# Wide and narrow products of one chunk in turns: the order of a four-step block of matmuls

## The chip, the cores and the metric

The kernel runs on one core of a Trainium2 chip. The metric is the device time of one launch in microseconds (us), the median of several runs. The profile is of one execution of the same program; its own time is given beside its span.

## The reference

Two transformer-like blocks are applied to 256 tokens of width 2048, in float32. The part that matters here is that nearly all of the work is products of a weight matrix with the activations:

```
# first block                              # second block
proj = h @ w_in            (2048 -> 3072)  proj = h @ w_in_2           (2048 -> 11264)
y = concat(y_lru, y_pool) @ w_out          merged = sig_r * (o_ret @ w_ret_up) + sig_m * (o_moba @ w_moba_up)
x = x + gt1 * y                            x = x + merged @ w_out_2
f = (silu(h @ w_ffn_gate)                  f = gated, convolved (h @ w_ffn_up_2)
     * (h @ w_ffn_up)) @ w_ffn_down             @ w_ffn_down_2
x = x + gt2 * f                            x = x + f ; final norm
```

Between them lie norms, a modulation from a vector c (`c_act @ w_ada`), a short convolution, a gated recurrence, a pooling mixer, and in the second block retention and block attention over the same 256 tokens. The feed-forward width is 5632.

## The kernel before

Activations are feature-major: a tile such as `h_s` is 128 partitions x 16 blocks x 2 halves x 256 tokens. The two halves are the high part of a number in the fp32r format (half 0) and the rest of it (half 1). Weights are treated the same way: each weight is split into a high and a low part, and a product of a weight with an activation is taken as high x high, high x low and low x high.

**Slabs and chunks.** A weight matrix is worked on in slabs of 256 output columns. A slab is two blocks of 128 columns (`b` = 0, 1), and its contraction is cut into four chunks of `kt` blocks of 128 (`kt` is 4, and 3 in the last group of the feed-forward down-projection). SP's queue loads the chunk into `raw`. ACT writes its high part into the tile `split` (`convert`, L902), DVE subtracts and writes the low part (L1241) and counts up `lo_ready`. `split` is a ring of four slots; ACT waits for `chunk_used`, which the last product of a chunk counts up, before it writes over a slot.

**Products.** `multiply` does one chunk. The accumulator is `ps[:, s, b, :]`: slab parity `s` and block `b` select one of four PSUM banks of 512 numbers. For each k and b there are two products. The *wide* one has the high weights as its stationary operand and both halves of the activations as its 512 moving columns; it writes the whole bank. The *narrow* one has the low weights and the high half of the activations, 256 columns, and writes the first half of the same bank. After the slab ACT copies the second half out (L909) and DVE adds it to the first (L1254, L1256). In the slabs of values (`tok`, L560 and L567) weights and activations change places.

Before, a step of k is: wide of block 0, wide of block 1, narrow of block 0, narrow of block 1:

```
for b in range(2):
    pe.matmul(ps[:, s, b, :], ...512 columns..., start=start, stop=False)
for b in range(2):
    mm = pe.matmul(ps[:, s, b, 0:T], ...256 columns..., start=False, stop=stop)
```

**Who calls it.** `half_slab` (first projection, two chunks at a time), `slab` (nearly everything), the merge loop of the second block (moving operands `o_r` and `o_m`), and `first_pair`, the first two slabs of the first feed-forward part: there PE waits before each k for `h_ready`, since the activations are normalized block by block on DVE and ACT (L1370, L1375) while the products already run. All others wait ahead of a chunk. The last slab before each of two norms is done by `closing` (L648 to L650) instead, which has three narrow products for each k and b, all to one bank: in chunks 0 to 2 b changes after every three, in the last chunk all of block 0 come first. `closing` is not touched. Between chunks `ride_along` puts in products of the modulation (L591, L599, L611).

Of the kernel before, what the change touches and what calls it, by code (L numbers as in the profile page):

```python
# [29 lines left out]
P = 128  # L30
T = 256
D = 2048
DB = D // P
SLAB = 256
# [105 lines left out]
def build(nc, dram, out):  # L140
# [3 lines left out]
    def at(name, shape, offset, dt=F32):  # L144
        return nc.alloc_sbuf_tensor_at(name, shape, dt, offset=offset)

    top = 16512
    def place(size):
        nonlocal top
        where, top = top, top + size  # L150
        return where

    raw = at("raw", [P, RAW, KT, SLAB], place(RAW * KT * SLAB * 4))
    split = at("split", [P, RING, KT, 2, SLAB], place(RING * KT * 2 * SLAB * 4), F32R)
# [91 lines left out]
    ps = ctx.enter_context(nc.psum_tensor("ps", [P, 2, 2, 512], F32))  # L246
# [289 lines left out]
    def _(pe):  # L536
        def slab(S, s, acts, kt=KT, guard=None, tok=False, rides=False, after=None):

            if not (isinstance(S, int) and S < 2):
                pe.wait_ge(evacuated, evac_count_of(S) - 1)  # L540
            for c in range(CHUNKS):
                if guard is not None:
                    guard(c)
                multiply(CHUNKS * S + c, c, s, acts, c * kt, kt, c == 0, c == CHUNKS - 1, tok)
                if rides:
                    ride_along(CHUNKS * S + c)
                if after is not None:
                    after(c)

        def multiply(G, slot, s, acts, k0, kt, first, last, tok=False, ready=None):  # L550


            pe.wait_ge(lo_ready, G + 1)
            for k in range(kt):
                if ready is not None:
                    pe.wait_ge(h_ready, ready + k + 1)
                start, stop = first and k == 0, last and k == kt - 1
                for b in range(2):
                    if tok:
                        pe.matmul(ps[:, s, b, :], acts[:, k0 + k, 0, b * P:(b + 1) * P],  # L560
                                  split[:, slot, k, :, :].rearrange("p h n -> p (h n)"), start=start, stop=False)
                    else:
                        pe.matmul(ps[:, s, b, :], split[:, slot, k, 0, b * P:(b + 1) * P],  # L563
                                  acts[:, k0 + k, :, :].rearrange("p h t -> p (h t)"), start=start, stop=False)
                for b in range(2):
                    if tok:
                        mm = pe.matmul(ps[:, s, b, 0:SLAB], acts[:, k0 + k, 1, b * P:(b + 1) * P],  # L567
                                       split[:, slot, k, 0, :], start=False, stop=stop)
                    else:
                        mm = pe.matmul(ps[:, s, b, 0:T], split[:, slot, k, 1, b * P:(b + 1) * P],  # L570
                                       acts[:, k0 + k, 0, :], start=False, stop=stop)
            mm.then_inc(chunk_used, 1)

        offset = [HALF_SLABS]
# [141 lines left out]
        def half_slab(E, after=None):  # L716

            if E >= 2:
                pe.wait_ge(evacuated, E - 1)
            for c in range(2):  # L720
                k0 = KT * (2 * (E // HALF_SLABS) + c)
                if E % HALF_SLABS == 0:
                    pe.wait_ge(h_ready, k0 + KT)
                multiply(2 * E + c, (2 * E + c) % RING, E % 2, h_s, k0, KT, c == 0, c == 1)
                ride_along(2 * E + c)
# [24 lines left out]
        def first_pair(gu):  # L750

            for i in range(2 * CHUNKS):
                G, s, c = CHUNKS * gu + i, i % 2, i // 2
                if c == 0:
                    pe.wait_ge(evacuated, evac_count_of(gu + s) - 1)
                multiply(G, G % RING, s, h_s, c * KT, KT, c == 0, c == CHUNKS - 1,
                         ready=DB + c * KT if s == 0 else None)
# [93 lines left out]
        for q in range(IN2_SLABS):  # L851
# [4 lines left out]
            if q == 2:  # L856
# [3 lines left out]
                for b in range(2):  # L860
                    mm = pe.matmul(pm[3][:, b:b + 1], rstd_h[:, b * P:(b + 1) * P], ident[:, 0:1], start=True, stop=True)
# [1155 lines left out]
```

## Time and profile before

| | |
|---|---|
| median of 3 runs | 2596.44 us (2596.14 to 2596.61) |
| the profiled execution | 2596.39 us |
| its span | 2594.3 us |
| PE busy | 2527.9 us, 97% |
| weight loads (PEld) | 2147.6 us, 83% |
| DVE, ACT busy | 1781.3 us (69%), 1179.6 us (45%) |
| DMA | mean 214 GB/s |

PE is TensorE's matmul row and PEld its weight-load row; every matmul has a weight load of its own. Starts of matmuls are recorded, their ends are modelled, so the time from one start to the next tells how fast they go, and durations don't. Rows of several instructions give the start of the first.

### The profile page before, as it was taken

The page shows a single profiled execution, that of the slowest core. Times are in us where ns is not written, and L with a number is a line of the kernel's source. Part 1 is how long each engine was busy: PE and PEld are TensorE (multiplying, and loading weights), DVE is VectorE, ACT ScalarE, POOL GpSimd, SP SyncE. Part 2 cuts the span into 40 slices and gives each one's busy share as a digit, 9 for nine tenths or more (in the row PEclk, how much of TensorE's full clock was granted, in tenths as well). Part 3 has the DMA queues.
Part 4 walks back from the last instruction along what each step waited for, and adds up shares of the span by engine and source line. Part 5 has one row for each costly group of instructions (what it writes and reads, how often), then busy time and mean ns, then how long its engine had stood idle before and what let it go on. Part 6 is the DMA issues. An engine that isn't in the chain of part 4 may idle for free.

```text
span 2594.3 us, 39845 instructions
## 1 busy us (share of the span) xinstructions
PE 2527.9 (97%) x14556; PEld 2147.6 (83%) x14556; DVE 1781.3 (69%) x2300; ACT 1179.6 (45%) x1439; POOL 17.5 (1%) x52
## 2 busy tenths in 40 slices
PE   4999999999999999999999999999999999999998
PEld 0666788888888888888888888888888888888887
DVE  2568698955555555688686665576788668876886
ACT  1345345444444444564454554445544444444444
POOL 1000000000000000000000000000000000000000
PEclk8999999999999999999999999999999999999999
DMA  9978987955555555566555455556555655555554
GB/s 372 402 273 325 381 336 261 355 179 190 191 186 187 191 188 186 165 194 201 188 172 172 163 176 188 188 184 195 177 181 184 204 185 192 186 189 181 190 167 125
DMA packets 156809, 554.48 MB, mean 214 GB/s; under 512 B 16400, under 2 KB 20496, under 8 KB 156704
## 3 DMA queue, kind: packets, MB, share of 16 engines
q1 hardware_dynamic: 155376, 549.85, 61.8%
q0 software_dynamic: 1328, 3.21, 0.4%
q8 instruction: 68, 1.11, 0.2%
q14 instruction: 37, 0.30, 0.0%
HBM read 550.37 MB, written 2.10 MB: 213 GB/s over the span
## 4 chain that ended last, share of the span: by engine, by line
PE 90%; DVE 4%; DMA 3%; ACT 1%; issue 1%; SPq 0%; DVEq 0%; ACTq 0%
PE ps L563 55%; PE ps L570 27%; DMA ride<-in_w_ada 3%; PE ps L560 2%; PE pm L591 2%; DVE split L1241 1%; PE ps L567 1%; ACT split L902 1%; DVE acc_out L1294 0%; PE pm L611 0%; DVE x_t L1397 0%; PE pm L712 0%; DVE val L1254 0%; DVE val L1370 0%; DVE h_s L1596 0%
## 5 line engine op out<-in xcount | busy, mean ns | idle before, releaser
L1241 DVE TENSOR_TENSOR split<-raw,split 128x1024 fp32r<-128x1024 f32 (+1 forms) x864 | 1030.8, 1203 | 686.1 <-ACT split L902 682.6
L902 ACT ACTIVATE split<-raw 128x1024 fp32r<-128x1024 f32 (+1 forms) x864 | 896.1, 1043 | 1138.7 <-PE ps L570 1081.0
L563 PE MATMUL ps<-h_s,split 128*128 128x512 f32 x3880 | 1231.0, 399 | 14.3 <-DVE split L1241 6.4
L570 PEld LDWEIGHTS ps<-h_s,split 128*128 128x128 f32 x3880 | 731.1, 188 | 173.0
L570 PE MATMUL ps<-h_s,split 128*128 128x256 f32 x3880 | 764.6, 278 | 0.0
L563 PE MATMUL ps<-mid_s,split 128*128 128x512 f32 x2336 | 737.3, 397 | 0.5 <-DVE split L1241 0.4
L563 PEld LDWEIGHTS ps<-h_s,split 128*128 128x128 f32 x3880 | 594.5, 189 | 43.0 <-issue 35.7
L570 PEld LDWEIGHTS ps<-mid_s,split 128*128 128x128 f32 x2336 | 440.2, 188 | 104.2
L570 PE MATMUL ps<-mid_s,split 128*128 128x256 f32 x2336 | 460.0, 278 | 0.0
L563 PEld LDWEIGHTS ps<-mid_s,split 128*128 128x128 f32 x2336 | 356.7, 189 | 7.4 <-issue 5.2
L909 ACT ACTIVATE low<-ps 128x512 f32<-128x512 f32 x230 | 133.2, 579 | 0.0
L591 PE MATMUL pm<-ride,c_act 128*1 128x512 f32 x512 | 75.9, 667 | 36.1 <-DMA ride<-in_w_ada 36.1
L1254 DVE TENSOR_TENSOR val<-ps,low 128x512 f32<-128x512 f32 x126 | 86.1, 683 | 1.2 <-ACT low L909 1.1
L1682 DVE SCALAR_TENSOR_TENSOR conv_o<-up_pad,par,conv_o 128x256 f32<-128x256 f32 x176 | 77.5, 482 | 11.4 <-DVE conv_o L1680 5.6
L560 PE MATMUL ps<-split,h_s 128*128 128x512 f32 x256 | 80.9, 397 | 0.0
L1256 DVE TENSOR_TENSOR low<-ps,low 128x512 f32<-128x512 f32 x88 | 60.2, 684 | 0.2
L591 PEld LDWEIGHTS pm<-ride,c_act 128*1 128x1 f32 x512 | 6.8, 81 | 62.6 <-DMA ride<-in_w_ada 37.4
L567 PEld LDWEIGHTS ps<-split,h_s 128*128 128x128 f32 x256 | 48.1, 188 | 11.4
L567 PE MATMUL ps<-split,h_s 128*128 128x256 f32 x256 | 50.3, 278 | 0.0
L1100 ACT ACTIVATE conv_o<-conv_o 128x512 f32<-128x512 f32 x22 | 13.9, 634 | 65.4 <-DVE conv_o L1682 65.4
L563 PE MATMUL ps<-o_m,split 128*128 128x512 f32 x128 | 40.3, 396 | 0.0
L563 PE MATMUL ps<-o_r,split 128*128 128x512 f32 x128 | 40.2, 395 | 0.0
(267 smaller groups left out, 1196.3 us busy)
## 6 DMA issues: line engine op xcount, KB each, us to landing
raw<-in_w_in SPq DMA_DIRECT2D x224, 512.0 KB, 3.5
ride<-in_w_ada SPq DMA_DIRECT2D x64, 1024.0 KB, 8.3
raw<-in_w_ffn_down SPq DMA_DIRECT2D x128, 512.0 KB, 4.2
raw<-in_w_ffn_gate SPq DMA_DIRECT2D x88, 512.0 KB, 4.2
raw<-in_w_ffn_up SPq DMA_DIRECT2D x88, 512.0 KB, 4.2
raw<-in_w_ffn_a SPq DMA_DIRECT2D x88, 512.0 KB, 3.7
raw<-in_w_ffn_b SPq DMA_DIRECT2D x88, 512.0 KB, 4.4
raw<-in_w_out SPq DMA_DIRECT2D x64, 512.0 KB, 5.4
```

The costliest lines, as they stand in the source:

```text
L560: pe.matmul(ps[:, s, b, :], acts[:, k0 + k, 0, b * P:(b + 1) * P], split[:, slot, k, :, :].rearrange("p h n -> p (h n)"), start=start, sto ...
L563: pe.matmul(ps[:, s, b, :], split[:, slot, k, 0, b * P:(b + 1) * P], acts[:, k0 + k, :, :].rearrange("p h t -> p (h t)"), start=start, sto ...
L567: mm = pe.matmul(ps[:, s, b, 0:SLAB], acts[:, k0 + k, 1, b * P:(b + 1) * P], split[:, slot, k, 0, :], start=False, stop=stop)
L570: mm = pe.matmul(ps[:, s, b, 0:T], split[:, slot, k, 1, b * P:(b + 1) * P], acts[:, k0 + k, 0, :], start=False, stop=stop)
L591: mm = pe.matmul(pm[2 + n % 2][g:g + 1, :], c_act[:, k:k + 1], src[:, e, 512 * h:512 * h + 512], start=(i == 0), stop=(i == PIECES - 1))
L902: act.activation(split[:, c, 0:kt, 0, :], raw[:, CHUNKS * s + c, 0:kt, :], ACT.Copy).then_inc(hi_ready, 1)
L909: act.activation(low[:, s, :, :], ps[:, s, :, T:2 * T], ACT.Copy).then_inc(low_copied, 1)
L1100: act.activation(conv_o[:, 0, :, :], conv_o[:, 0, :, :], ACT.Silu).then_inc(act_done, 1)
L1241: dve.tensor_tensor(split[:, c, 0:kt, 1, :], raw[:, CHUNKS * s + c, 0:kt, :], split[:, c, 0:kt, 0, :].bitcast(F32), ALU.subtract).then_inc ...
L1254: ins = dve.tensor_tensor(dst, ps[:, s, :, 0:T], both, ALU.add)
L1256: own(dve.tensor_tensor(both, ps[:, s, :, 0:T], both, ALU.add))
L1682: ins = dve.scalar_tensor_tensor(out=dst, in0=src, scalar=w, in1=dst, op0=ALU.mult, op1=ALU.add)
```

## The change

In a chunk, the order of the same products. One loop over k takes the wide product of block 0 and the narrow one of block 1; a second loop takes the wide product of block 1 and the narrow one of block 0. The wide product that opens a bank's sum (`start`) must come before any narrow one to that bank, so in the first chunk of a slab the wide one of block 1 for k = 0 is taken ahead of everything, and in the second loop the wide ones of block 1 run one k ahead (`k + 1`), with none beside the last narrow one. `mm.then_inc(chunk_used, 1)` stays on the chunk's last product. The waits for `h_ready` are in the first loop only.

```
+            def wide(b, k):
+                start, stop = first and k == 0, last and b == 1 and k == kt - 1
+                ...
+            def narrow(b, k):
+                stop = last and b == 0 and k == kt - 1
+                ...
             for k in range(kt):
                 if ready is not None:
                     pe.wait_ge(h_ready, ready + k + 1)
-                start, stop = first and k == 0, last and k == kt - 1
-                for b in range(2):
-                    ...wide...  start=start, stop=False
-                for b in range(2):
-                    ...mm = narrow...  start=False, stop=stop
+                if k == 0 and first:
+                    wide(1, 0)
+                wide(0, k)
+                narrow(1, k)
+            for k in range(kt):
+                if not first:
+                    wide(1, k)
+                elif k + 1 < kt:
+                    wide(1, k + 1)
+                mm = narrow(0, k)
             mm.then_inc(chunk_used, 1)
```

With W for wide, N for narrow and the block behind it, four k of a later chunk go from `W0 W1 N0 N1` four times to `W0 N1` four times and then `W1 N0` four times; a slab's first chunk becomes `W1 W0 N1 W0 N1 W0 N1 W0 N1 W1 N0 W1 N0 W1 N0 N0`.

## Rows read from the trace of the kernel before

**Rows 1.** The page: busy times, the chain that ended last, the converts of DVE

```profile
PE 2527.9 (97%) x14556; PEld 2147.6 (83%) x14556; DVE 1781.3 (69%) x2300; ACT 1179.6 (45%) x1439; POOL 17.5 (1%) x52
...
PE 90%; DVE 4%; DMA 3%; ACT 1%; issue 1%; SPq 0%; DVEq 0%; ACTq 0%
PE ps L563 55%; PE ps L570 27%; DMA ride<-in_w_ada 3%; PE ps L560 2%; PE pm L591 2%; DVE split L1241 1%; PE ps L567 1%; ACT split L902 1%; DVE acc_out L1294 0%; PE pm L611 0%; DVE x_t L1397 0%; PE pm L712 0%; DVE val L1254 0%; DVE val L1370
...
L1241 DVE TENSOR_TENSOR split<-raw,split 128x1024 fp32r<-128x1024 f32 (+1 forms) x864 | 1030.8, 1203 | 686.1 <-ACT split L902 682.6
```

**Rows 2.** Waits of PE: total us, times, longest us

```profile
PE pm L591 <- DMA ride<-in_w_ada: 36.1, 18, 19.5
PE ps L563 <- DVE split L1241: 6.8, 3, 6.1
...
PE ps L563 <- DVE h_s L1375: 2.5, 1, 2.5
```

**Rows 3.** Stretches: busy us of each engine (instructions), granted clock, DMA share, GB/s

```profile
600.00:1000.00 400.00, 400.00 (x2299) 349.02 (x2299) 228.51 (x240) 175.40 (x191) 0.00 (x0) 1.00 0.57 189
...
396.00:399.00 3.00, 3.00 (x10) 2.52 (x11) 3.00 (x9) 2.03 (x4) 0.00 (x0) 0.50 0.37 143
```

**Rows 4.** Groups of PE by line and form: count, busy us, mean ns, idle before

```profile
L563 PE MATMUL ps<-h_s,split 128*128 128x512 f32 x3880 | 1231.0, 399 | 14.3 <-DVE split L1241 6.4 <-issue 3.1 <-DVE h_s L1375 2.5
L570 PE MATMUL ps<-h_s,split 128*128 128x256 f32 x3880 | 764.6, 278 | 0.0
L563 PE MATMUL ps<-mid_s,split 128*128 128x512 f32 x2336 | 737.3, 397 | 0.5 <-DVE split L1241 0.4
...
L560 PE MATMUL ps<-split,h_s 128*128 128x512 f32 x256 | 80.9, 397 | 0.0
...
L563 PE MATMUL ps<-o_m,split 128*128 128x512 f32 x128 | 40.3, 396 | 0.0
L563 PE MATMUL ps<-o_r,split 128*128 128x512 f32 x128 | 40.2, 395 | 0.0
```

**Rows 5.** PE in order of time, steady stretch: start us, us, what

```profile
1600.14 0.63 PE L563 MATMUL ps<-h_s,split 128*128 128x512 f32 x2
1600.61 0.39 PE L570 MATMUL ps<-h_s,split 128*128 128x256 f32 x2
1600.84 0.63 PE L563 MATMUL ps<-h_s,split 128*128 128x512 f32 x2
...
1611.29 0.63 PE L563 MATMUL ps<-h_s,split 128*128 128x512 f32 x2
```

**Rows 6.** PE in order of time at the lower clock

```profile
397.23 1.05 PE L563 MATMUL ps<-h_s,split 128*128 128x512 f32 x2
398.09 0.63 PE L570 MATMUL ps<-h_s,split 128*128 128x256 f32 x2
398.51 1.05 PE L563 MATMUL ps<-h_s,split 128*128 128x512 f32 x2
```

**Rows 7.** Single products and weight loads of one step, in order of time

```profile
1499.65 0.40 PE L563 MATMUL ps<-h_s,split 128*128 128x512 f32 x1
...
1499.88 0.19 PEld L570 LDWEIGHTS ps<-h_s,split 128*128 128x128 f32 x1
...
1499.88 0.40 PE L563 MATMUL ps<-h_s,split 128*128 128x512 f32 x1
1500.12 0.28 PE L570 MATMUL ps<-h_s,split 128*128 128x256 f32 x1
1500.12 0.19 PEld L570 LDWEIGHTS ps<-h_s,split 128*128 128x128 f32 x1
...
1500.23 0.19 PEld L563 LDWEIGHTS ps<-h_s,split 128*128 128x128 f32 x1
...
1500.35 0.62 PE L563 MATMUL ps<-h_s,split 128*128 128x512 f32 x2
```

**Rows 8.** The closing slab of the end: first and last products of 72

```profile
2572.77 0.28 PE L648 MATMUL ps<-h_s,split 128*128 128x256 f32 x1
2572.89 0.28 PE L649 MATMUL ps<-h_s,split 128*128 128x256 f32 x1
...
2581.28 0.28 PE L650 MATMUL ps<-h_s,split 128*128 128x256 f32 x1
```

**Rows 9.** The merge loop, steps that read o_m: first and eighth

```profile
1667.72 0.63 PE L563 MATMUL ps<-o_m,split 128*128 128x512 f32 x2
...
1672.66 0.63 PE L563 MATMUL ps<-o_m,split 128*128 128x512 f32 x2
```

**Rows 10.** DVE in order of time while first_pair begins

```profile
395.18 0.48 DVE L1375 SCALAR_TENSOR_TENSOR h_s<-val,mod,h_s 128x256 fp32r<-128x256 f32 x1 [0.18 <-ACT h_s L967]
...
395.98 0.48 DVE L1375 SCALAR_TENSOR_TENSOR h_s<-val,mod,h_s 128x256 fp32r<-128x256 f32 x1
...
396.76 0.48 DVE L1375 SCALAR_TENSOR_TENSOR h_s<-val,mod,h_s 128x256 fp32r<-128x256 f32 x1
...
397.55 0.48 DVE L1375 SCALAR_TENSOR_TENSOR h_s<-val,mod,h_s 128x256 fp32r<-128x256 f32 x1
```

More of the change, by code:

```diff
@@ L553, in multiply @@
             pe.wait_ge(lo_ready, G + 1)
+            def wide(b, k):
+                start, stop = first and k == 0, last and b == 1 and k == kt - 1
+                if tok:
+                    return pe.matmul(ps[:, s, b, :], acts[:, k0 + k, 0, b * P:(b + 1) * P],
+                                     split[:, slot, k, :, :].rearrange("p h n -> p (h n)"), start=start, stop=stop)
+                return pe.matmul(ps[:, s, b, :], split[:, slot, k, 0, b * P:(b + 1) * P],
+                                 acts[:, k0 + k, :, :].rearrange("p h t -> p (h t)"), start=start, stop=stop)
+            def narrow(b, k):
+                stop = last and b == 0 and k == kt - 1
+                if tok:
+                    return pe.matmul(ps[:, s, b, 0:SLAB], acts[:, k0 + k, 1, b * P:(b + 1) * P],
+                                     split[:, slot, k, 0, :], start=False, stop=stop)
+                return pe.matmul(ps[:, s, b, 0:T], split[:, slot, k, 1, b * P:(b + 1) * P],
+                                 acts[:, k0 + k, 0, :], start=False, stop=stop)
             for k in range(kt):
@@ L556, in multiply @@
                     pe.wait_ge(h_ready, ready + k + 1)
-                start, stop = first and k == 0, last and k == kt - 1
-                for b in range(2):
[L559 to L564, printed above, removed]
-                for b in range(2):
[L566 to L571, printed above, removed]
+                if k == 0 and first:
[8 more added lines that the diff above has]
+                mm = narrow(0, k)
             mm.then_inc(chunk_used, 1)
```

## The prediction

> **What bounds the kernel now.** I read the page first. TensorE is busy for 97% of the span and makes 90% of the chain that ended last, and nearly all of that chain is the lines of `multiply`: L563 and L570, and L560 and L567 for the token-major slabs [rows 1]. The waits of PE come next. The longest total is 36.1 us on the DMA of the early modulation weights; waits for a split chunk come to 6.8 us, and for a normalized block to 2.5 us [rows 2]. None is inside the long stretch: between 600 and 1000 us PE is busy for all 400 us at granted clock 1.00 [rows 3]. So the time is set by how fast TensorE takes one product after another, and I look at the starts of products, because their ends are modelled.
>
> The change acts on wide products (512 columns) and narrow ones (256). The grouped lines give 3880 + 2336 + 128 + 128 + 256 = 6728 wide ones and as many narrow ones [rows 4], so there are 3364 steps of k with two wide and two narrow products each. In the steady stretch a pair of wide ones starts at 1600.14, its pair of narrow ones at 1600.61, and the pair of wide ones 16 steps on at 1611.29: 11.15 / 16 = 0.697 us a step, 0.47 of it for the wide pair and 0.23 for the narrow pair [rows 5]. 3364 x 0.697 = 2345 us of the 2594.3 us span lies in such steps. The smallest change that a measurement can tell from none, 0.2% or 5.2 us, is 5.2 / 3364 = 1.5 ns a step. The question is whether the order moves a step of 697 ns by 1.5 ns.
>
> **What a step is made of.** At the start of the first feed-forward part the granted clock is 0.50 [rows 3], the 1.2 GHz level, and there the step takes 398.51 - 397.23 = 1.28 us [rows 6]. At the 2.4 GHz level half of that, 640 ns, would be its pure column work; it takes 697. So 57 ns a step are not column work, 14 for each product. Where in the order do they sit? Two views help. The single starts show a weight load with each product, and each load starts when the product before it starts (loads at 1499.88, 1500.12 and 1500.23, in each case at the start of a product) [rows 7]: one load ahead, never two. The other view is the closing slab, which is narrow products only: 71 intervals from 2572.77 to 2581.28 make 8.51 / 71 = 0.120 us each [rows 8], which is 107 of column work (a sixth of 640 ns: 256 of 1536 columns) and 13 more. That row also holds the bank question: there three products in a row write one bank, and in the last chunk twelve do, at the same 0.12 us. Four products at 13 ns make 53 of the 57. About 4 ns a step (between 3 and 5 by the rounding of these rows) are peculiar to the mixed step, and these can hang on order.
>
> **The change, part by part.**
> *Instructions.* The same 16 products of a chunk of four k, with the same operands, starts and stops and the same single signal at the end: 14556 matmuls before and after. Nothing is removed or added. 0 us.
>
> *Banks.* The title says that neighbours shall write different banks. They do already: before, the order is bank 0, 1, 0, 1 in every step and across steps. After, they alternate inside each of the two loops, but the narrow one of block 1 that ends the first loop is followed in a later chunk by a wide one of block 1, and the chunk ends on block 0 where the next chunk of the slab begins; in a slab's first chunk the last two narrow ones both write block 0. So same-bank neighbours rise from none to two or so a chunk. By the closing slab such a neighbour costs nothing [rows 8]. I take 0 us; as a bound, even 4 ns on each of 2 x 856 neighbours would be 6.8 us (864 converted chunks [rows 1], less the eight of the two closing slabs, which don't use `multiply`).
>
> *Loads.* Before, the loads under a step's four products are those of a wide, narrow, narrow and wide one; all are 128x128. After, each wide product covers the load of a narrow one and each narrow one that of a wide one. Both orders have two loads a step under wide products (0.235 us each) and two under narrow ones (0.115). With one load ahead [rows 7] and all loads alike, the sum is the same. 0 us.
>
> A rule bears on this: the Trainium skill, "TensorE: Matmul & The Clock Gate", section "Back-to-back issue gap", gives a warm isolated product its columns over 2.4 GHz and about 2.5 ns, whatever stands beside it. An estimate from that page is 650 ns for a step in either order; the trace disagrees with the size (697) and says nothing against the independence of order. By the page the sum is again 0 us.
>
> *Width changes.* Before, a step has two changes of width (wide to narrow, narrow to wide) and after it four. The trace of before holds all four kinds of neighbours. Starts are 0.23 after a wide one that follows narrow, 0.24 after the wide one ahead of narrow, 0.11 to 0.12 after a narrow one [rows 7]; the kind of neighbour moves an interval by no more than the 10 ns that a row can show. So it isn't excluded that the 4 ns peculiar to the mixed step belong to one kind. If they belong to the wide products as such, 0. If to the two width changes, they double: +4 x 3364 = +13.5 us. If to a wide one behind a wide one, or to a narrow one behind a narrow one in the mixed step, they go: -13.5 us. I take the first, because each product's load and columns are what they were, and the rows show the wide interval as 0.23 to 0.24 in both surroundings.
>
> *Addresses.* One row shows that a step can depend on what else it reads: with o_m as the moving operand, seven steps take 1672.66 - 1667.72 = 4.94, or 706 ns each [rows 9], 9 more than with h_s. The new order pairs other loads with other moving operands, so up to 9 x 3364 = 30 us bounds this from above. The two tiles h_s and mid_s, with which nearly all steps run, show no such thing in either pair of a step, so I take 0.
>
> *Blocks that arrive one by one.* Only `first_pair` waits inside a chunk. After, the second half of a chunk runs behind the last wait. There DVE finishes a block every 0.79 us (395.18, 395.98, 396.76, 397.55) [rows 10], and the clock is at 1.2 GHz. After, the first loop takes 1.07 us for k = 0 (two wide ones at a third of 1.28, 0.427, and a narrow one at a sixth, 0.213) and 0.64 for each further one: it would want k = 1 to 3 at 396.9, 397.5 and 398.2, and they are there by about 396.5, 397.2 and 398.0 (start plus 0.48). PE doesn't wait. 0 us, at most 0.1. Elsewhere the waits come ahead of the whole chunk. The converts on ACT and DVE wait for a chunk's last product, which stays where it was; so do the copies out of `ps`.
>
> Sum: 2594.3 + 0 of the span, and the profiled execution, 2596.39, stands 2.1 above its span and at the median of the runs, 2596.44. Forecast 2596.5.
>
> **The rivals.**
> *No effect (forecast), 2596.5; own range 2591 to 2602.* For it: same loads, same columns, one load ahead, alternating banks before. This is also the case in which the change doesn't do what it says. Chance 0.52.
>
> *Width changes cost, 2610.* The mixed step's 4 ns sit at the two changes of width and become 8. For it: the interval ahead of the narrow pair is the longest wide one, 0.24 [rows 7]; a queue that has just loaded under a short product may start the long one late. Against it: narrow to wide is no longer than narrow to narrow. It decides from 1.5 ns a step. With the address effect on top it could reach 2626. Chance 0.22.
>
> *Spacing out the narrow ones helps, 2583.* With two narrow products in a row, two loads running lie under short products; in turns, each load under a short product comes after one under a long product, in which the queue can get ahead. For it: loads back to back all the way, as in the closing slab, run at 0.120 an interval where the mixed step's narrow pair has 0.115 each, so a narrow product does go faster after wide ones [rows 5, 8]. A gain of 4 ns a step is 13.5 us. If each narrow interval fell to the shortest shown, 0.11, it would be 2 x 5 x 3364 = 34 us, 2563. Against it: the total of a step need not fall when a start moves. Chance 0.26.
>
> **How the numbers follow.** The three cases are also the three outcomes, since each rival's price is over twice the 0.2%: same 0.52, slower 0.22, faster 0.26. The range takes in both rivals at their 13.5 us with some 2 to 3 us for the rounding of the 4 ns: 2580 to 2613. Outside are the extremes, the address effect and narrow intervals at their floor, about 1 in 10 each.
>
> **What would show it right or wrong.** Right: 16 steps of k in the steady stretch again take 11.15 us, whatever the order inside; wide intervals 0.23 to 0.24, narrow ones 0.115; ACT and DVE wait for PE as before. The slower rival shows as wide intervals of 0.24 throughout or narrow ones of 0.12, with every chunk of four k longer than 2.79 us. The faster one shows as narrow intervals of 0.11 at the same wide ones. If bank neighbours mattered, the interval at a chunk's middle and end would stand out from the rest. The prediction is wrong if the step's 57 ns depend on which product a load lies under, which no row of before can show, since its order is the same everywhere.

## The result and the profile after

The changed kernel takes 2609.33 us (median of 5 runs, 2608.06 to 2611.08), against 2596.44 for the kernel before (5 runs, 2595.33 to 2596.80): a ratio of 1.0047, with a 95% interval of 1.0036 to 1.0058. It is slower by about 13 us. The time lies in the range of the prediction and beside the 2610 us of its slower rival. The case that the prediction held to be the likeliest, no effect, did not come.

The page after, beside [rows 1]:

```profile
span 2607.8 us, 39845 instructions
...
PE 2542.6 (97%) x14556; PEld 2155.6 (83%) x14556; DVE 1781.5 (68%) x2300; ACT 1180.9 (45%) x1439; POOL 17.4 (1%) x52
```

The number of products is the same, and the other engines work as long as before. Only PE has more. Its waits, beside [rows 2], haven't grown:

```profile
PE pm L604 <- DMA ride<-in_w_ada: 34.9, 17, 20.3
PE ps L561 <- DVE split L1254: 6.7, 3, 6.1
...
PE ps L561 <- DVE h_s L1388: 2.5, 1, 2.5
```

So nobody keeps PE waiting longer. The stretches, beside [rows 3], at the same granted clock:

```profile
600.00:1000.00 400.00, 400.00 (x2284) 348.35 (x2283) 227.33 (x241) 173.83 (x188) 0.00 (x0) 1.00 0.57 187
```

PE gets 2284 products done in the 400 us where it did 2299: 0.66% fewer. The loss is in the intervals themselves, and it is not spread evenly. PE in order of time, at the starts of three slabs (the two wide products in a row mark a slab's first chunk):

```profile
743.01 0.63 PE L561 MATMUL ps<-h_s,split 128*128 128x512 f32 x2
...
754.15 0.63 PE L561 MATMUL ps<-h_s,split 128*128 128x512 f32 x2
...
765.45 0.63 PE L561 MATMUL ps<-h_s,split 128*128 128x512 f32 x2
...
967.41 0.63 PE L561 MATMUL ps<-h_s,split 128*128 128x512 f32 x2
```

One slab takes 11.14 us and the next 11.30. Before, 16 steps take 11.15 [rows 5]. The 20 slabs from 743.01 to 967.41 average 11.22. Inside the first of the two, in a later chunk, eight pairs of a wide and a narrow product, that is four steps of k, go by in 2.77 us (746.18 to 748.95). Inside the second they take 2.83 us (759.43 to 762.26):

```profile
746.18 0.39 PE L561 MATMUL ps<-h_s,split 128*128 128x512 f32 x1
...
748.95 0.39 PE L561 MATMUL ps<-h_s,split 128*128 128x512 f32 x1
...
759.43 0.40 PE L561 MATMUL ps<-h_s,split 128*128 128x512 f32 x1
759.68 0.28 PE L569 MATMUL ps<-h_s,split 128*128 128x256 f32 x1
759.80 0.40 PE L561 MATMUL ps<-h_s,split 128*128 128x512 f32 x1
760.03 0.28 PE L569 MATMUL ps<-h_s,split 128*128 128x256 f32 x1
760.14 0.40 PE L561 MATMUL ps<-h_s,split 128*128 128x512 f32 x1
760.38 0.28 PE L569 MATMUL ps<-h_s,split 128*128 128x256 f32 x1
760.50 0.40 PE L561 MATMUL ps<-h_s,split 128*128 128x512 f32 x1
...
762.26 0.40 PE L561 MATMUL ps<-h_s,split 128*128 128x512 f32 x1
```

The same alternation of the same products on the same tiles has two rhythms. In the fast one a step takes 2.77 / 4 = 0.693 us, less than the 0.697 of before. In this chunk of the slow one it takes 0.708. The rows are rounded to 0.01 us, but the trace holds the starts to 1 ns: the slow rhythm goes in a cycle of three pairs, with wide intervals of 241, 235 and 234 ns and narrow ones of 121, 113 and 116; in the fast one wide intervals are 230 to 233 ns and narrow ones 112 to 117. What puts a slab into one or the other is the matter of the experiments.

### The profile page after: what moved, and what is told of

Its sections match the earlier page's. It is cut to its first block, busy times and chain, and to the rows that moved or that the text cites. A ratio compares the mean times of both kernels' runs of the same rounds, so it can differ in the third digit from the quotient of the medians.

```text
span 2607.8 us, 39845 instructions
## 1 busy us (share of the span) xinstructions
PE 2542.6 (97%) x14556; PEld 2155.6 (83%) x14556; DVE 1781.5 (68%) x2300; ACT 1180.9 (45%) x1439; POOL 17.4 (1%) x52
## 4 chain that ended last, share of the span: by engine, by line
PE 92%; DVE 3%; DMA 3%; issue 1%; ACT 1%; SPq 0%; DVEq 0%; ACTq 0%
PE ps L561 55%; PE ps L569 28%; DMA ride<-in_w_ada 3%; PE ps L559 2%; PE pm L604 2%; PE ps L567 1%; DVE acc_out L1307 1%; DVE split L1254 1%; ACT split L915 0%; PE pm L624 0%; PE pm L725 0%; PE pm L612 0%; PE ps L661 0%; DVE val L1267 0%; PE ps L662 0%
## 5 line engine op out<-in xcount | busy, mean ns | idle before, releaser
L561 PE MATMUL ps<-h_s,split 128*128 128x512 f32 x3880 | 1368.9, 400 | 14.2 <-DVE split L1254 6.4
L569 PE MATMUL ps<-h_s,split 128*128 128x256 f32 x3880 | 1067.6, 281 | 0.0
L561 PEld LDWEIGHTS ps<-h_s,split 128*128 128x128 f32 x3880 | 724.7, 189 | 204.9 <-issue 37.5
L561 PE MATMUL ps<-mid_s,split 128*128 128x512 f32 x2336 | 815.9, 397 | 0.3 <-DVE split L1254 0.3
L569 PEld LDWEIGHTS ps<-h_s,split 128*128 128x128 f32 x3880 | 735.7, 190 | 12.0
L569 PE MATMUL ps<-mid_s,split 128*128 128x256 f32 x2336 | 641.8, 280 | 0.0
L561 PEld LDWEIGHTS ps<-mid_s,split 128*128 128x128 f32 x2336 | 433.6, 188 | 105.4 <-issue 6.0
L569 PEld LDWEIGHTS ps<-mid_s,split 128*128 128x128 f32 x2336 | 441.1, 189 | 6.9
L559 PE MATMUL ps<-split,h_s 128*128 128x512 f32 x256 | 89.8, 398 | 0.0
L567 PE MATMUL ps<-split,h_s 128*128 128x256 f32 x256 | 70.3, 280 | 0.0
L559 PEld LDWEIGHTS ps<-split,h_s 128*128 128x128 f32 x256 | 47.6, 188 | 10.7
L567 PEld LDWEIGHTS ps<-split,h_s 128*128 128x128 f32 x256 | 48.3, 189 | 0.7
```

Of the source, the lines that this page charges most:

```text
L559: return pe.matmul(ps[:, s, b, :], acts[:, k0 + k, 0, b * P:(b + 1) * P], split[:, slot, k, :, :].rearrange("p h n -> p (h n)"), start=sta ...
L561: return pe.matmul(ps[:, s, b, :], split[:, slot, k, 0, b * P:(b + 1) * P], acts[:, k0 + k, :, :].rearrange("p h t -> p (h t)"), start=sta ...
L567: return pe.matmul(ps[:, s, b, 0:SLAB], acts[:, k0 + k, 1, b * P:(b + 1) * P], split[:, slot, k, 0, :], start=False, stop=stop)
L569: return pe.matmul(ps[:, s, b, 0:T], split[:, slot, k, 1, b * P:(b + 1) * P], acts[:, k0 + k, 0, :], start=False, stop=stop)
```

## The experiments

In all of them but the last two, `multiply` walks through a list `plan` of (wide or narrow, block, k), with the same calls `wide` and `narrow`, the same `start` on the first product of each bank's sum and the signal on the chunk's last product. Only the list is shown. Each time is the median of 4 to 11 runs (one for `wideonly`), and its ratio is to 17 to 33 runs of the kernel before in the same session; one execution of each was profiled. A step's length is read from starts of products in the steady stretch; its loss is what it has above 693.3 ns, for a reason that `wideonly` gives.

**1. Alternate without a break (pairs).**

```diff
+plan = [(kind, b, k) for k in range(kt) for b in range(2) for kind in "wn"]      # W0 N0 W1 N1
```

> Order in every chunk W0 N0 W1 N1 for each k: wide and narrow alternate without a break, also across first chunks, and each pair writes one bank. After shows two rhythms of the alternating order, some 693.5 and some 707.5 ns per step of k, that change from slab to slab where the first chunk has two wide and two narrow ones in a row. Two-rhythm theory: with no such seam one rhythm stays, so nearly all slabs are fast (about 2596.5 - 3364 x 3.2 ns = 2586 us) or nearly all slow (about 2596.5 + 3364 x 10.8 ns = 2633 us), not half and half. Width-change theory (2 ns for each change of width, four a step): 2610 us, every step about 701 ns. Bank theory (after lost its 13 us at some 2.5 same-bank neighbours a chunk, 6 ns each): two such neighbours a step, 2596.5 + 3364 x 2 x 6 ns = 2637 us.

2607.01 us (2598.26 to 2618.36), ratio 1.0032 (1.0017 to 1.0047). The spread is the finding: 20 us between runs, where before has 5.4 in the same sessions. The profiled execution took 2618.36 us and is slow for the whole stretch from 600 to 1000 us:

```profile
600.00:1000.00 400.00, 400.00 (x2266) 346.83 (x2265) 225.78 (x238) 171.81 (x186) 0.00 (x0) 1.00 0.56 185
```

That is 1.4% fewer products than before, every slab alike: by starts to 1 ns, all 142 whole chunks of four k in this stretch take 705 to 708 ns a step, 706.7 on average. The change from slab to slab is gone with the two wide and two narrow ones in a row. This also answers a rival: the other engines' work differs between the two slabs of a pair (in the changed kernel 8 DVE instructions from 743.0 to 754.1 us, 5 from 754.1 to 765.4), and here both kinds of slab keep one rhythm. One rhythm for a whole run, 2586 or 2633, was expected too, and that didn't come.

**2. The same, banks as in the change (noseam).**

```diff
+k0_ = 1 if first else 0
+plan = [(kind, b, 0) for b in range(2) for kind in "wn"] if first else []
+plan += [p for k in range(k0_, kt) for p in (("w", 0, k), ("n", 1, k))]
+plan += [p for k in range(k0_, kt) for p in (("w", 1, k), ("n", 0, k))]
```

> As the changed kernel, but a slab's first chunk begins W0 N0 W1 N1 for k = 0 and then goes on W0 N1 and W1 N0, so there are never two of one width in a row; same-bank neighbours stay a few a chunk. Two-rhythm theory: no switching from slab to slab; 2586 us if the rhythm that stays is the fast one, 2633 us if the slow one. Width-change theory: 2610 us. Bank theory: 2610 us as well, since the count of same-bank neighbours hardly changes.

2603.44 us (2596.68 to 2616.78), ratio 1.0021 (1.0012 to 1.0031), again with a spread of 20 us. The profiled execution (2616.78 us) shows why. Its stretches:

```profile
600.00:1000.00 400.00, 400.00 (x2267) 346.93 (x2266) 226.00 (x240) 172.70 (x187) 0.00 (x0) 1.00 0.56 185
...
1800.00:2020.00 220.00, 219.59 (x1242) 190.16 (x1242) 173.58 (x241) 105.75 (x126) 0.00 (x0) 1.00 0.55 184
2320.00:2500.00 180.00, 180.00 (x1040) 157.38 (x1039) 126.77 (x167) 78.85 (x86) 0.00 (x0) 1.00 0.57 189
```

and those of before:

```profile
1800.00:2020.00 220.00, 219.51 (x1260) 191.38 (x1259) 178.02 (x251) 105.58 (x124) 0.00 (x0) 1.00 0.55 185
2320.00:2500.00 180.00, 180.00 (x1036) 157.04 (x1035) 130.37 (x176) 78.85 (x86) 0.00 (x0) 1.00 0.55 181
```

The first two stretches are slow from end to end (2267 products for 2299, 1242 for 1260). The last is fast, faster than before (1040 for 1036). So a rhythm holds for hundreds of microseconds and changes at a few places in a run. What changes it there is not known. That the spread of both kernels' runs comes from which rhythm is held for how long fits the profiled executions, which are the slowest of their ten runs; the faster runs have no trace.

**3. Banks alone (samebank).**

```diff
+plan = [p for k in range(kt) for p in (("w", 0, k), ("w", 1, k), ("n", 1, k), ("n", 0, k))]
```

> The order before with its narrow ones exchanged: W0 W1 N1 N0 for each k. Widths in the same order as before, but two same-bank neighbours a step (W1 N1, N0 W0) where before had none. Bank theory: 2637 us, or at least clearly above 2600. Two-rhythm and width-change theory: banks don't matter, 2596.5 us.

2597.48 us (2594.25 to 2599.32), ratio 0.9997 (0.9987 to 1.0006). Two same-bank neighbours in every step cost nothing that these runs or the traces show; the step is 696.7 ns in both. The bank theory falls, and with it the aim that the prediction names for the change ("neighbours shall write different banks"): there was nothing to gain from different banks.

**4. Fewer changes of width (fours).**

```diff
+plan = [(kind, b, k) for j in range(0, kt, 2) for kind in "wn" for k in range(j, min(j + 2, kt)) for b in range(2)]
```

> Two k together: W0 W1 W0 W1 N0 N1 N0 N1, always alternating banks, half as many changes of width as before (one a step). Width-change theory: 2596.5 - 3364 x 2 ns = 2590 us. Bank theory: 2596.5 us. Two-rhythm theory: no forecast of the size; narrow ones in a row drift toward the closing slab's 0.120 us, so up to 3364 x 4 ns = 13 us slower, 2600 to 2610 us.

2608.47 us (2607.49 to 2608.83), ratio 1.0043 (1.0029 to 1.0057). Half the changes of width, and as slow as the change under study. A price for each change of width, whatever stands around it, is out. PE in order of time:

```profile
804.47 1.09 PE L567 MATMUL ps<-h_s,split 128*128 128x512 f32 x4
805.40 0.64 PE L575 MATMUL ps<-h_s,split 128*128 128x256 f32 x4
...
808.68 1.09 PE L567 MATMUL ps<-h_s,split 128*128 128x512 f32 x4
```

Six steps take 4.21 us, 0.702 each, of which four wide ones take 0.93 and four narrow ones 0.48, that is 0.12 apiece as in the closing slab [rows 8].

**5. Wide products by themselves (wideonly).** The narrow products, so the part with the low weights, are left out.

```diff
+plan = [("w", b, k) for k in range(kt) for b in range(2)]
```

> The narrow products are left out (no low-weight part), the wide ones stay: measures the interval of wide products by themselves. If the 4 ns peculiar to the mixed step belong to wide products as such, 228.5 ns; if wide and narrow ones share a fixed 13.3 ns beside their columns, 226.7 ns; if the wide interval is what the starts of before show, 233 ns. The whole time falls to some 1500 to 1900 us, set by PE and in places by the converts on DVE (1.2 us a chunk against 1.83 us of products).

2129.89 us, one run. The whole time was forecast too low: PE now waits 142 us for `split`. The interval is what was asked for. In a run without waits, from the first to the twenty-sixth product:

```profile
1023.62 6.28 PE L565 MATMUL ps<-split,h_s 128*128 128x512 f32 x27
...
1029.29 0.61 PE L565 MATMUL ps<-split,h_s 128*128 128x512 f32 x2
```

5.67 / 25 = 0.2268 us. So a wide product among wide ones takes 213.3 + 13.4 ns and a narrow one among narrow ones 106.7 + 13.2 [rows 8]. Two of each make 693.3 ns. That is the fast rhythm's step, to the rounding of the rows. The fast rhythm has no loss; before (696.7 ns) loses 3.3 ns a step and the slow rhythm (706.7 on average) 13.

**6. An old first chunk, then alternate (oldfirst).**

```diff
+if first:
+    plan = [(kind, b, k) for k in range(kt) for kind in "wn" for b in range(2)]
+else:
+    plan = [p for k in range(kt) for p in (("w", 0, k), ("n", 1, k))]
+    plan += [p for k in range(kt) for p in (("w", 1, k), ("n", 0, k))]
```

> A slab's first chunk in the order of before (two wide, two narrow), the other chunks W0 N1 four times, then W1 N0 four times. Two-rhythm theory: the order before has one rhythm (696.7 ns a step), so the alternating part is always entered alike, and all slabs come out alike, with little spread between runs: if it falls into the fast rhythm 2596.5 - 2520 x 3.2 ns = 2588 us, if into the slow one 2596.5 + 2520 x 10.8 ns = 2624 us; slabs that alternate between the two, as after has them, would speak against it. Width-change theory (already contradicted by the eight-product order): 2596.5 + 2520 x 4 ns = 2607 us.

2604.92 us (2599.49 to 2611.97), ratio 1.0034 (1.0023 to 1.0046). A spread of 12 us, so the entry is not the same each time: the order of before doesn't set the rhythm. It carries it along. The profiled execution (2599.49 us) held the fast one for the 400 us and kept it through every first chunk: 2307 products.

```profile
600.00:1000.00 400.00, 400.00 (x2307) 349.59 (x2306) 229.26 (x242) 175.51 (x192) 0.00 (x0) 1.00 0.59 189
...
2040.00:2300.00 260.00, 260.00 (x1479) 225.83 (x1478) 192.23 (x262) 113.63 (x124) 0.00 (x0) 1.00 0.55 186
```

Later in the same execution the slow one is carried in the same way, from 2040 to 2300 us, with 1479 products where before has 1492:

```profile
2040.00:2300.00 260.00, 259.90 (x1492) 226.62 (x1491) 195.60 (x267) 113.44 (x124) 0.00 (x0) 1.00 0.55 185
```

**7. The old order for one k in each chunk (oldstep).**

```diff
+plan = [(kind, b, 0) for kind in "wn" for b in range(2)]
+plan += [p for k in range(1, kt) for p in (("w", 0, k), ("n", 1, k))]
+plan += [p for k in range(1, kt) for p in (("w", 1, k), ("n", 0, k))]
```

> In every chunk k = 0 in the order of before, then the other three k alternating. Two-rhythm theory: the rhythm is set anew in each chunk, so it can't stay slow or fast by the history of a slab; if each chunk falls into the fast one 2588 us, if into the slow one 2624 us, and little spread between runs either way. Width-change theory: 2607 us.

2603.75 us (2602.51 to 2605.52), ratio 1.0024 (1.0015 to 1.0033). Little spread, as expected, but not one rhythm for all chunks. In order of time, starts of three chunks (the first wide pair of each):

```profile
2341.11 0.63 PE L569 MATMUL ps<-h_s,split 128*128 128x512 f32 x2
...
2343.93 0.63 PE L569 MATMUL ps<-h_s,split 128*128 128x512 f32 x2
...
2346.70 0.63 PE L569 MATMUL ps<-h_s,split 128*128 128x512 f32 x2
```

2.82 us, then 2.77: the break turns one rhythm into the other chunk by chunk, as the first chunk of the change does slab by slab, and the average is half and half again.

**8. Both kinds of neighbours in each two k (twos).**

```diff
+# for each two k, j and j + 1:
+plan += [("w", 0, j), ("w", 1, j), ("n", 0, j), ("w", 0, j + 1),
+         ("n", 1, j), ("w", 1, j + 1), ("n", 0, j + 1), ("n", 1, j + 1)]
```

> Two k together as W W N W N W N N: one wide pair and one narrow pair in eight products, banks alternating except at one place. Width-change theory (2 ns each, three a step where before has two): 2603 us. Two-rhythm theory: an arrangement with its own single rhythm, the same in every slab and with little spread between runs; its step lies between 693.5 and 707.5 ns, so 2586 to 2633 us, no better forecast.

2623.16 us (2621.35 to 2624.39), ratio 1.0094 (1.0078 to 1.0109), the slowest. The same in every slab, with a step of (809.75 - 804.10) / 8 = 0.706 us:

```profile
804.10 0.63 PE L573 MATMUL ps<-h_s,split 128*128 128x512 f32 x2
...
809.75 0.63 PE L573 MATMUL ps<-h_s,split 128*128 128x512 f32 x2
```

**9. Eight and eight (eights).**

```diff
+plan = [(kind, b, k) for kind in "wn" for k in range(kt) for b in range(2)]
```

> In each chunk all eight wide products, then all eight narrow ones, banks alternating. A step in products of one width alone costs 2 x 226.7 + 2 x 120.0 = 693.3 ns (measured with wide ones only and in the closing slab); the loss beside it is 3.3 ns a step in the order of before and 8.7 ns in the order of fours, 17 ns for each group of four wide and four narrow. Loss-at-the-change theory: about the same 17 ns once a chunk, 4.3 ns a step, 2600 us. If the loss came from narrow ones in a row as such, it would grow with their number: 2610 us or more.

2602.76 us (2600.98 to 2605.90), ratio 1.0022 (1.0013 to 1.0031). Three chunks take 8.38 us:

```profile
798.26 2.00 PE L567 MATMUL ps<-h_s,split 128*128 128x512 f32 x8
...
806.64 2.00 PE L567 MATMUL ps<-h_s,split 128*128 128x512 f32 x8
```

0.698 a step, 5 ns of loss, or 20 ns a chunk where fours loses 17 in each of its groups. Long runs of narrow ones as such cost nothing more. The starts to 1 ns show where the 20 ns lie. From 600 to 1000 us the first five wide products behind narrow ones take 233, 235, 229, 232 and 231 ns on average, and from the sixth on it is 226 to 227 as in `wideonly`. The first two narrow ones behind wide ones take 113 and 118 ns, less than the 120 of the others, and give back a part.

**10. Sixteen and sixteen (mirror).**

```diff
+mirrored = slot % 2 == 1 and not first
+plan = [(kind, b, k) for kind in ("nw" if mirrored else "wn") for k in range(kt) for b in range(2)]
```

> As eights, but every second chunk takes its narrow products first and then its wide ones, so the runs of one width are 16 long across chunks and a width changes once a chunk instead of twice. Loss-at-the-change theory: half of what eights loses, some 9 ns a chunk or 2.2 ns a step, 2596.5 - 3364 x 1.1 ns = 2593 us, with little spread between runs. If no loss beside the pure 693.3 ns were left, 2586 us.

2597.39 us (2595.79 to 2600.20), ratio 1.0005 (0.9996 to 1.0014). The step came out as forecast, 11.14 / 16 = 0.696:

```profile
792.08 3.82 PE L568 MATMUL ps<-h_s,split 128*128 128x512 f32 x16
...
797.65 3.82 PE L568 MATMUL ps<-h_s,split 128*128 128x512 f32 x16
...
803.22 3.82 PE L568 MATMUL ps<-h_s,split 128*128 128x512 f32 x16
```

The time did not: the 3.5 us that were expected below before don't show in the runs. The steady stretch isn't the whole run: over all whole chunks of four k in the two traces a step is 697.2 ns against 697.7 before, and 3364 x 0.5 ns are 1.7 us, too little to tell. No order that was tried beats the order of before.

**11 and 12. Addresses (shift32, shift64).** The order of before, all tiles of SBUF moved up.

```diff
-    top = 16512
+    top = 16512 + 32        # shift64: + 64
```

> The order of before, all tiles of SBUF moved up by 32 bytes, so h_s and mid_s lie as o_m does now (32 bytes past a multiple of 64) and o_m at a multiple of 64. Address theory: the merge steps on o_m, up to 707 ns before, go to 697 and all other steps from 697 to some 700 to 707, so 2605 to 2630 us. Otherwise 2596.5 us, and o_m stays the odd one.

> Control for the shift: the order of before, all tiles moved up by 64 bytes, so every tile keeps its place to a multiple of 64. Both theories: 2596.5 us, o_m steps as before.

2597.29 us, ratio 1.0002 (0.9993 to 1.0011), and 2598.77 us, ratio 1.0004 (0.9994 to 1.0013). No effect. With o_m at a multiple of 64 its steps are still the long ones, (1670.22 - 1666.68) / 5 = 0.708 us, as in [rows 9]:

```profile
1666.68 0.63 PE L563 MATMUL ps<-o_m,split 128*128 128x512 f32 x2
...
1670.22 0.63 PE L563 MATMUL ps<-o_m,split 128*128 128x512 f32 x2
```

The address theory falls in this form. Why the merge steps on o_m are longer stays open. It is not the loop: in the kernel before, the eight steps with o_r that follow those of [rows 9] are of the same loop and as many to a slab, and take (1678.95 - 1673.37) / 8 = 0.698 us:

```profile
1673.37 0.63 PE L563 MATMUL ps<-o_r,split 128*128 128x512 f32 x2
...
1678.95 0.63 PE L563 MATMUL ps<-o_m,split 128*128 128x512 f32 x2
```

## Why the prediction was right and wrong

**What bounds the kernel** was right: PE takes products back to back, no wait changed, and 3364 steps carry the whole effect. (11.22 - 11.15) / 16 is 4.4 ns a step, and 3364 of them are 15 us, by rows that are rounded to 0.01 us. By starts to 1 ns, over all whole chunks of four k in the two traces, a step is 701.4 ns after and 697.7 before, and 3364 x 3.7 ns are 12.4 us; 13 were measured.

**Banks at 0** was right, as was the finding that neighbours wrote different banks already: samebank, 0.9997. **Blocks that arrive one by one at 0** fits the unchanged waits of PE. **Addresses at 0** was right in the sum, and a shift of all tiles changes nothing either.

**Loads at 0** rested on a sum: the same loads under products of the same lengths. The sum is right for the fast rhythm only, 693 ns. It doesn't hold for the slow one, where the same loads under the same products take 13 ns a step more. The prediction also leaned on the Trainium skill, "TensorE: Matmul & The Clock Gate", "Back-to-back issue gap", and read more into it than it says: the formula of columns over 2.4 GHz and 2.5 ns is given there for an isolated product, and for a stream of weight loads and products the same section says that both set the spacing. These runs show that columns alone don't: wide intervals of one order and one operand run from 230 to 242 ns in the changed kernel, and the orders of the same products that were tried took from 2597 to 2623 us.

**The step that failed** is *width changes*, "I take the first", that is 0 because the roughly 4 ns peculiar to the mixed step belong to the wide products as such. They do not. Wide products by themselves take 226.7 ns, so in the order of before 3.3 ns a step are lost in the mixing. The estimate of 4 ns was nearly right; the place was wrong. So the mechanism of the forecast failed, and that 2609.33 us lies in the range is due to the rival that was priced into it.

**The slower rival** had the right number, 2610, by a mechanism that is only half right, so its number is luck. It charged each of four changes of width alike, which makes every step 701 ns. What happens is 693 in most of one slab and 704 to 709 in the next; their mean is 701 by the accident that the first chunk's two wide and two narrow ones in a row switch the rhythm once a slab. Where that break is gone a rhythm stays for hundreds of microseconds (noseam: 2596.68 to 2616.78). And fours, with half the changes, should then have gained 7 us; it lost 11. **The faster rival** is also half there: the fast rhythm does bring a step to below 697, through narrow ones spaced out.

**Two rhythms** is shown, by the after trace and by pairs, noseam, oldfirst and oldstep. That mixed widths lose time and runs of one width don't is shown by wideonly, the closing slab, eights and mirror. What sets the loss is not. The steps, by starts to 1 ns, averaged over the whole chunks of four k from 600 to 1000 us (the fast rhythm from 1200 to 1300 us in `noseam`):

| order | changes of width in a chunk | a step, ns | loss in a chunk, ns |
|---|---|---|---|
| alternating, fast rhythm (noseam) | 16 | 693.3 | 0 |
| alternating, slow rhythm (pairs) | 16 | 706.7 | 53 |
| twos | 12 | 706.7 | 53 |
| before, samebank | 8 | 696.7 | 13 |
| fours | 4 | 701.7 | 33 |
| eights | 2 | 698.3 | 20 |
| mirror | 1 | 695.8 | 10 |

From four changes downward the loss goes with their number, though not in proportion, and `eights` shows where it lies: in the first five wide products behind narrow ones. Above four it does not go with their number. What in the chip holds a rhythm, a load's readiness against the end of the product before it or a queue's pace, was not separated, and no order was found that picks the fast one. Held all through it would give about 2596.5 - 3364 x 3.3 ns = 2585 us, an estimate that no run reached.

## What to carry to other kernels

Where one engine runs back to back, compare the interval of each kind of instruction among its own kind with its interval in the mix: the difference, here 3.3 ns in 697, is an estimate of what an order can win. Here it took one run with the narrow products left out, and no order that was tried had shorter steps on average than that sum. An order of alternating long and short instructions can have more than one stable rhythm, so look at several slabs and at several runs before taking one interval for the whole; a spread of 20 us where the kernel before has 5 is such a sign. Before spacing writes over PSUM banks, look whether they alternate already and whether a same-bank neighbour costs anything.

## What the hardware showed that was not expected

The same alternation of wide and narrow matmuls, on the same tiles and at the same granted clock (1.00), ran at 693.3 or at 706.7 ns for two wide and two narrow ones, for hundreds of microseconds at a time within one execution (noseam). Its runs spread from 2596.68 to 2616.78 us; that they differ in which rhythm they hold is inferred, since one was profiled. A break of two wide or two narrow ones in a row turns one rhythm into the other in some orders (after, oldstep), and the order two and two, kept for a chunk, passes it on unchanged (oldfirst). At granted clock 1.00, a matmul in the fp32r format with a weight load each took 226.7 ns for 512 columns and 120 ns for 256 among neighbours of its own width, by the estimate of the prediction 13.3 ns more than its columns. Behind narrow ones it took five wide products until that interval was reached (eights, mirror).
